# Seven products in place of eight for six K-tile pairs of the last down projection

## The reference

```python
def conv_ffn(h, w_up, conv_w, conv_b, w_down):     # D_MODEL 2048, D_FF 5632
    u = causal_depthwise_conv(h @ w_up, conv_w, conv_b)
    val, gate = jnp.split(u, 2, axis=-1)
    return (jax.nn.gelu(gate) * val) @ w_down      # (256 x 5632) @ (5632 x 2048), added to x
```

## Time and profile before

| | |
|---|---|
| three runs | 2272.08, 2274.09, 2274.53 us (median 2274.09) |
| span of the profiled execution, first to last instruction | 2272.6 us |
| own time of the profiled execution | not listed apart from the runs; the median is 1.5 us above its span |
| last section, first matmul | 2029.93 us from the start of the span |
| TensorE busy, mean granted clock | 2264.1 us (100%), 0.999 |
| VectorE, ScalarE, GpSimd busy | 1502.4, 1268.4, 619.1 us |

### The profile page before, as it was taken

The page is one execution under the profiler, slowest core; times in us unless marked ns, Lnnn a source line. Parts: engine busy times, 40 slices in busy tenths (PEclk is TensorE's granted clock), DMA queues, the critical chain, the costliest instruction groups (busy, mean ns, idle before and its releaser), DMA issues.

```text
span 2272.6 us, 33897 instructions
## 1 busy us (share of the span) xinstructions
PE 2264.1 (100%) x11072; PEld 1911.0 (84%) x11072; DVE 1502.4 (66%) x1812; ACT 1268.4 (56%) x1663; POOL 619.1 (27%) x1027
## 2 busy tenths in 40 slices
PE   9999999999999999999999999999999999999999
PEld 7888888988888888888888888898888888888887
DVE  6766775676767667665556778658767767665443
ACT  6655664565556555544444777556655655554333
POOL 0720001234343343412221100215434344340000
PEclk9999999999999999999999999999999999999999
DMA  8655435547776776766665555636867676776555
GB/s 274 207 199 200 133 126 176 176 151 219 217 223 214 222 222 213 222 206 202 203 203 188 174 193 175 200 126 216 253 220 221 216 223 212 221 221 193 194 193 167
DMA packets 143779, 455.24 MB, mean 200 GB/s; under 512 B 25888, under 2 KB 26784, under 8 KB 143696
## 3 DMA queue, kind: packets, MB, share of 16 engines
q1 hardware_dynamic: 117696, 420.40, 58.0%
q0 software_dynamic: 25856, 33.65, 4.9%
q10 hardware_dynamic: 144, 0.06, 0.0%
HBM read 423.73 MB, written 2.10 MB: 187 GB/s over the span
## 4 chain that ended last, share of the span: by engine, by line
PE 99%; ACT 0%; DVE 0%; DMA 0%; issue 0%; SPq 0%; ACTq 0%
PE ps L412 50%; PE ps L417 25%; PE ps L370 10%; PE ps L374 5%; PE ps L355 2%; PE ps L391 2%; PE ps L729 1%; PE ps L978 1%; PE ps L715 0%; PE ps L809 0%; PE ps L698 0%; PE ps L637 0%; DMA xT<-in_x_t 0%; PE ps L691 0%; PE ps L830 0%
## 5 line engine op out<-in xcount | busy, mean ns | idle before, releaser
L343 DVE TENSOR_TENSOR w_lo<-raw,w_hi 128x1024 fp32r<-128x1024 f32 x788 | 978.8, 1245 | 702.4 <-ACT w_hi L337 699.6
L337 ACT ACTIVATE w_hi<-raw 128x1024 fp32r<-128x1024 f32 x787 | 830.8, 1059 | 855.7 <-PE ps L417 738.7
L412 PE MATMUL ps<-w_hi,xg_hl 128*128 128x512 f32 (+1 forms) x3392 | 832.9, 388 | 1.9 <-DVE xg_hl L1462 1.9
L412 PEld LDWEIGHTS ps<-w_hi,xg_hl 128*128 128x128 f32 x3392 | 631.8, 188 | 131.4 <-DVE xg_hl L1462 2.4
L417 PE MATMUL ps<-w_lo,xg_hl 128*128 128x512 f32 (+1 forms) x1696 | 450.1, 388 | 0.0
L412 PE MATMUL ps<-w_hi,a_hl 128*128 128x512 f32 x1656 | 411.9, 391 | 0.3 <-ACT vmem L1110 0.2
L417 PEld LDWEIGHTS ps<-w_lo,xg_hl 128*128 128x128 f32 x1696 | 317.0, 188 | 65.3
L412 PEld LDWEIGHTS ps<-w_hi,a_hl 128*128 128x128 f32 x1656 | 308.8, 188 | 65.0 <-issue 0.7
L2140 POOL DMA_DIRECT2D u_t<-z_t x704 | 346.5, 500 | 2.8 <-issue 2.8
L417 PE MATMUL ps<-w_lo,a_hl 128*128 128x512 f32 x828 | 221.4, 389 | 0.0
L417 PEld LDWEIGHTS ps<-w_lo,a_hl 128*128 128x128 f32 x828 | 155.4, 188 | 32.5
(11 more groups left out here) (215 smaller groups left out, 1779.2 us busy)
## 6 DMA issues: line engine op xcount, KB each, us to landing
raw<-in_w_stream SPq DMA_DIRECT2D x787, 512.0 KB, 4.2
u_t<-z_t POOLq DMA_DIRECT2D x704, 34.0 KB, 3.4
bias<-in_rel_bias POOLq DMA_DIRECT2D x4, 768.0 KB, 5.8
memT<-in_mem_t POOLq DMA_DIRECT2D x4, 512.0 KB, 6.0
gate_w<-in_gate_w POOLq DMA_DIRECT2D x4, 512.0 KB, 3.8
x_tok<-x_turned SPq DMA_DIRECT2D x16, 128.0 KB, 4.3
out_t<-x_tok SPq DMA_DIRECT2D x8, 256.0 KB, 4.3
u_dn<-z_dn POOLq DMA_DIRECT2D x48, 32.0 KB, 3.2
```

What stands on the lines that cost most here:

```text
L337: nc.scalar.activation(w_hi[:, s, :], raw[:, s, :], ACT.Copy).then_inc(hi_done, 1)
L343: nc.vector.tensor_tensor(w_lo[:, s, :], raw[:, s, :], w_hi[:, s, :].bitcast(F), ALU.subtract).then_inc(lo_done, 1)
L412: nc.tensor.matmul(ps[:, bank + tt, 0:n], a[:, k0 + k, tt * P:tt * P + P], w_hi[:, s, k * n:k * n + n], start=start and k == 0 and q == 0, ...
```

## The change

For six of the 22 pairs (pairs 0 to 5, K-tiles 0 to 11) the two column blocks of a half q (blocks 2q and 2q+1) are computed together. The 2 x 2 x 2 = 8 block products (two token halves, two K-tiles, two column blocks) are replaced by the seven products of a Winograd form. GpSimd makes sums and differences of the activations' token halves (`forms`, three batches of two pairs each: one instruction that adds `a_hi` and `a_lo` over 1024 elements, then four over 256), ScalarE and VectorE split them. VectorE makes the sums of weight tiles (`weight_sums`, four instructions of 512). A paired step has four splits in place of two: one whole unit, half a unit and two summed tiles, and 21 matmuls in place of 24. After each half VectorE adds four more PSUM banks to the result (`product_sums`), with one copy by ScalarE. The units are reordered (`LAST_ORDER`): in the first half pairs 6 to 10 come first, then a paired step (`s`) after every two ordinary pairs (`c`, two units each); in the second half pairs 6 and 7 come first. Both blocks of a half now accumulate at the same time, block 2q in banks 0 and 1, block 2q+1 in banks 2 and 3, and the seven products in these and in banks 4 to 7.

```diff
+PAIRED = 6
+LAST_ORDER = [[("c", u) for u in range(6, 11)] + [x for j in range(5) for x in (("s", j), ("c", 11 + 2 * j), ("c", 12 + 2 * j))] + [("s", 5), ("c", 21)],
+              [("c", 6), ("c", 7)] + [x for j in range(PAIRED) for x in (("s", j), ("c", 8 + 2 * j), ("c", 9 + 2 * j))] + [("c", 20), ("c", 21)]]
+FORMS_AT = {6: 0, 14: 1, 22: 2}
...
+                if kind == "c":
+                    SPLITS += [("w", c), ("w", c + 1)]
+                else:
+                    SPLITS += [("w", c), ("h", c + 1), ("t", n, 0), ("t", n, 1)]
+                    RAW_OF[n] = c
...
+        SUMS_AT = {WSUM_SPLIT[PAIRED * (q + 1) - 1, 1] + SLOTS + j: (q, j) for q in range(2) for j in range(3)}
+        SUM_BEFORE = {SPLIT_OF[c]: n for n, c in RAW_OF.items()}
+        ADDS_AT = {e + b + SLOTS: (2 * q + b, e + b) for q, kind, u, e, _ in LAST if u == TOK_DOWN - 1 for b in range(2)}
...
+        def last_hi(act, e):
+            s, x = e % SLOTS, SPLITS[e - first["down1"]]
+            cols = slice(COLS if x[0] == "h" else 0, UE)
+            if x[0] == "t":
+                act.wait_ge(wsum_ready, 2 * x[1] + x[2] + 1)
+                src = t_raw[:, x[2], :]
+            else:
+                act.wait_ge(raw_full[x[1] % SLOTS], 16 * (x[1] // SLOTS + 1))
+                src = raw[:, x[1] % SLOTS, cols]
+            act.wait_ge(pe_unit, e - SLOTS + 1)
+            nc.scalar.activation(w_hi[:, s, cols], src, ACT.Copy).then_inc(hi_done, 1)
...
+                    if j % 2 == 0:
+                        pe.wait_ge(form_lo, min(n // 2, PAIRED // 2 - 1) + 1)
+                    if j == 0:
+                        if n:
+                            pe.wait_ge(sum_done, 1)
+                        else:
+                            pe.wait_ge(up_out, TT * 4 * UP_ITER)
+                    work = (((first_cols, a_part(0, 0), 4), (second_cols, a_part(1, 0), 0)),
+                            ((second_cols, s_part(3), 2),),
+                            ((first_cols, s_part(0), 5), (second_cols, s_part(1), 6)),
+                            ((first_cols, s_part(2), 7), (second_cols, a_part(1, 1), 1)))
+                    for x, products in enumerate(work):
+                        pe.wait_ge(hi_done, e + x + 1)
+                        for cols, form, bank in products:
+                            product(e + x, cols, form, bank, j == 0 and bank >= 4, False, None)
+                        pe.wait_ge(lo_done, e + x + 1)
+                        for cols, form, bank in products:
+                            last = product(e + x, cols, form, bank, False, j == PAIRED - 1 and bank >= 4, True)
+                        last.then_inc(pe_unit, 1)
...
+                for q, kind, u, e, n in LAST:
+                    if kind == "s":
+                        paired(u, e, n)
+                        continue
+                    begin, end = u == PAIRED, u == TOK_DOWN - 1
+                    for b in range(2):
+                        if q and b and end:
+                            continue
+                        token_unit(pe, e + b, 2 * u, 2, a_hi, a_lo, 2 * b, begin, end, value_there if q == 0 and b == 0 else None,
+                                   (lambda tt, b=b: pe.wait_ge(tile_done, 2 * b + tt + 1)) if q and begin else None)
...
+                last_hi(act, e)
+                if pos < 9:
+                    value_slot(1, UP_ITER, pos)
+                if pos in FORMS_AT:
+                    b = FORMS_AT[pos]
+                    act.wait_ge(form_made, b + 1)
+                    A(s_hl[:, 2 * b:2 * b + 2, :, 0, :].rearrange("p a f n -> p (a f) n"),
+                      s_f[:, 2 * b:2 * b + 2, :, 1, :].rearrange("p a f n -> p (a f) n"), ACT.Copy).then_inc(form_hi, 1)
...
+                ch.link(dve, V.tensor_tensor(t1, b12, b11, ALU.subtract))
+                V.tensor_tensor(t2, b22, t1, ALU.subtract).then_inc(wsum_ready, 1)
+                V.tensor_tensor(t3, b22, b12, ALU.subtract)
+                dve.wait_ge(wsum_ready, 2 * n + 1)
+                V.tensor_tensor(t4, b21, t2, ALU.subtract).then_inc(wsum_ready, 1)
...
+                if part == 0:
+                    dve.wait_ge(p1_out, q + 1)
+                    ch.link(dve, V.tensor_tensor(x_tok[:, n0, 0, :], x_tok[:, n0, 0, :], u_sum[:, :], ALU.add))
+                    ch.link(dve, V.tensor_tensor(u_sum[:, :], u_sum[:, :], ps[:, 6, :], ALU.add))
+                    ch.link(dve, V.tensor_tensor(x_tok[:, n1, 0, :], x_tok[:, n1, 0, :], u_sum[:, :], ALU.add))
+                if part == 1:
+                    ch.link(dve, V.tensor_tensor(u_sum[:, :], u_sum[:, :], ps[:, 7, :], ALU.add))
+                    x = x_tok[:, n0:n1 + 1, 1, :]
+                    ch.link(dve, V.tensor_tensor(x, x, u_sum[:, :].unsqueeze(1).to_broadcast([P, 2, COLS]), ALU.add))
+                if part == 2:
+                    x = x_tok[:, n1, :, :]
+                    ins = V.tensor_tensor(x, x, ps[:, 5, :].unsqueeze(1).to_broadcast([P, TT, COLS]), ALU.add)
+                    ins.then_inc(sum_done, 1)
+                    dve.wait_ge(sum_done, q + 1)
...
+                for e in range(c0 + SLOTS, END + SLOTS):
+                    pos = e - SLOTS - c0
+                    if e in SUMS_AT:
+                        q, part = SUMS_AT[e]
+                        dve.wait_ge(pe_unit, WSUM_SPLIT[PAIRED * (q + 1) - 1, 1] + 1)
+                        product_sums(q, part)
+                    if e in ADDS_AT and ADDS_AT[e][0] < 3:
+                        n, done = ADDS_AT[e]
+                        dve.wait_ge(pe_unit, done + 1)
+                        tile_adds(n)
+                    if e in SUM_BEFORE:
+                        weight_sums(SUM_BEFORE[e])
+                    if e < END:
+                        last_lo(dve, e)
+                    if pos < 9:
+                        value_slot(1, UP_ITER, pos)
+                    if pos in FORMS_AT:
+                        b = FORMS_AT[pos]
+                        dve.wait_ge(form_hi, b + 1)
+                        V.tensor_tensor(s_hl[:, 2 * b:2 * b + 2, :, 1, :].rearrange("p a f n -> p (a f) n"),
+                                        s_f[:, 2 * b:2 * b + 2, :, 1, :].rearrange("p a f n -> p (a f) n"),
+                                        s_hl[:, 2 * b:2 * b + 2, :, 0, :].rearrange("p a f n -> p (a f) n").bitcast(F), ALU.subtract).then_inc(form_lo, 1)
...
+            def forms(b):
+                if b == 0:
+                    pool.wait_ge(pe_unit, first["down1"])
+                    pool.wait_ge(g_lo, UP_ITER + PAIRED // 2)
+                ch.link(pool, G.tensor_tensor(a_f[:, 4 * b:4 * b + 4, :, 0, :],
+                                              a_hi[:, 4 * b:4 * b + 4, :].rearrange("p k (t n) -> p k t n", t=TT).bitcast(F),
+                                              a_lo[:, 4 * b:4 * b + 4, :].rearrange("p k (t n) -> p k t n", t=TT).bitcast(F), ALU.add))
+                a11, a21, a12, a22 = (s_f[:, 2 * b:2 * b + 2, f, 0, :] for f in range(4))
+                s1, s2, s3, s4 = (s_f[:, 2 * b:2 * b + 2, f, 1, :] for f in range(4))
+                ch.link(pool, G.tensor_tensor(s1, a21, a22, ALU.add))
+                ch.link(pool, G.tensor_tensor(s2, s1, a11, ALU.subtract))
+                G.tensor_tensor(s3, a11, a21, ALU.subtract)
+                G.tensor_tensor(s4, a12, s2, ALU.subtract).then_inc(form_made, 1)
+            def last_section():
+                for b in range(PAIRED // 2):
+                    forms(b)
...
+            down = down[[TOK_DOWN * (2 * q + b) + u for q in range(2) for _, u in LAST_ORDER[q] for b in range(2)]]
```

More of the change, by code:

```diff
@@ L145, in trunk @@
         rb = at("rb", top[0], [TT, P])
+        u_sum = at("u_sum", top[0], [COLS])
         sq = sb("sq", [SEQ])
@@ L269, in trunk @@
         out_done = sem("out_done")
+        form_made, form_hi, form_lo = sem("form_made"), sem("form_hi"), sem("form_lo")
+        wsum_ready, p1_out, sum_done = sem("wsum_ready"), sem("p1_out"), sem("sum_done")
         chains = {n: Chain(sem(f"{n}_self")) for n in ("act", "dve", "pool")}
@@ L281, in trunk @@
         N_UNITS = c
+        LAST, SPLITS, RAW_OF = [], [], {}
+        c, n = first["down1"], 0
+        for q in range(2):
+            for kind, u in LAST_ORDER[q]:
+                LAST.append((q, kind, u, first["down1"] + len(SPLITS), n))
+                if kind == "c":
[3 more added lines that the diff above has]
+                    RAW_OF[n] = c
+                    n += 1
+                c += 2
+        assert c == N_UNITS
+        END = first["down1"] + len(SPLITS)
+        SPLIT_OF = {x[1]: first["down1"] + j for j, x in enumerate(SPLITS) if x[0] != "t"}
+        WSUM_SPLIT = {(x[1], x[2]): first["down1"] + j for j, x in enumerate(SPLITS) if x[0] == "t"}
+        SUMS_AT = {WSUM_SPLIT[PAIRED * (q + 1) - 1, 1] + SLOTS + j: (q, j) for q in range(2) for j in range(3)}
+        SUM_BEFORE = {SPLIT_OF[c]: n for n, c in RAW_OF.items()}
```

(64 more changed lines are left out.)

22 lines of the change are left out of this document (11 added, 11 removed).

## The result

The changed kernel takes 2282.8 us (median of nine runs), the kernel before 2273.8 in runs beside it: ratio 1.0042, 95% interval 1.003 to 1.0053. That is 9.0 us more; 2283.0 was forecast. By that interval the change costs 6.8 to 12.1 us. The profiled execution took 2285.5 us, 2.7 more than the median (span 2283.8, mean granted clock 0.996).

What follows compares the result with a forecast made beforehand. The prediction took TensorE, busy all the span, to bound the kernel. -8.2 (matmuls) + 12.3 (start) + 1.75 (clock) + 3.0 (turn) = +8.9 on 2274.1 gave 2283.0 us, range 2269.5 to 2289.

Steps and rivals of the forecast that it cites:

- What goes: Twelve paired steps with 21 matmuls for 24: 36 matmuls fewer at 0.227 us each, -8.2 us.
- The regular stretch at nothing: In the cycles of a paired step and four ordinary units, slack of 1.7 us or more hides the added work: no cost.
- The start, +12.3: At the section's first paired step, VectorE and GpSimd alternate one instruction each, so TensorE starts it 12.3 us late.
- overlap (0.8): Rival at the start: the engines don't disturb each other, 0.8 us late and no clock loss, 2269.7 us in all; chance 0.13.
- VectorE keeping its turn (6.2): Rival at the start: VectorE keeps its turn while it has work, 6.2 us late, 2276.9 us in all; chance 0.15.
- The clock, +1.75: Behind the pause at the start the granted clock falls once, losing 1.75 us; bounds 0 and 3.5.
- The turn, +3.0: Between the halves TensorE waits for banks to be added, 2.1 us for block 0 and 0.9 for block 1: +3.0 us.
- The sum: Matmuls, start, clock and turn over the whole kernel: +8.9 us, giving 2283.0 us.

Runs made afterwards that it cites:

- cleared: `late_start` with the blocks' banks added first at the turn, GpSimd's batches and the forms' splits moved to where VectorE has slack: 2265.2 us, ratio 0.9964.
- spread_forms: Changed kernel with GpSimd's second and third batch of forms waiting for the section's 12th and 20th split: 2274.6 us, ratio 1.0001.
- late_spread_turn: `late_start` with the blocks' banks added first at the turn and GpSimd's later batches waiting as in `spread_forms`: 2269.0 us, ratio 0.9981.
- memset_forms: Changed kernel with GpSimd's fifteen forms instructions replaced by memsets of the same outputs, which read nothing (output wrong): 2269.1 us, ratio 0.998.
- filled_gap: Changed kernel with 50 matmuls whose result nobody reads run in the gap before the first paired step: 2279.8 us, ratio 1.003.
- late_start: Changed kernel with seven pairs in place of five ahead of the first half's first paired step: 2274.8 us, ratio 1.0009.

## Why the prediction was right

**What goes.** 36 matmuls, 8.2 us. Confirmed: the account closes with 8.16. In `cleared`, where nearly only this is left, the section is 6.1 us shorter with 2.05 of excess in it, and the medians are 7.5 apart.

**The regular stretch at nothing.** Confirmed: there is no wait in it afterwards, and the account leaves nothing over. The size of the slack was not measured; it held until `spread_forms` and `late_spread_turn` put GpSimd's batches into these cycles, and then TensorE waited.

**The start, +12.3.** Measured 11.91. The mechanism was the one named, turns of one instruction each: a pair of small instruction and multiply-add was put at 0.87, and eight multiply-adds with seven small and one long GpSimd instruction between them took 8.78, where the prediction's turns give 7 x 0.87 + 2.68 = 8.77. Two rivals fall by the trace of the changed kernel: overlap (0.8) and VectorE keeping its turn (6.2). `memset_forms` shows that GpSimd costs this only where it reads, and `spread_forms` that the cost hangs on where its batches fall.

The Trainium skill ("SBUF — State Buffer", section Who interferes with whom) says that a VectorE instruction with two inputs in SBUF meets a GpSimd instruction that reads SBUF, not one that only writes. Both halves agree with this case: 8.78 us against 3.25 for the same eight instructions.

**The clock, +1.75.** Right mechanism, size too small: 2.95 at the first paired step. It was taken from a stretch of the kernel's start that lost 1.75; here 2.95 lost at half the clock stand for 5.9 us at the low level (0.50 in the first two stretches above). `filled_gap` isolates it. The clock fell a second time, at the turn, which the sum doesn't have. Together both falls cost 4.6 us by my estimate (2.95, and 1.65 of the 1.83 at the turn, after about 0.18 of wait for the second bank as in `filled_gap`), more than the bound of 3.5.

**The turn, +3.0.** The first wait was 2.05, where the working gives 12.1 - 10.2 = 1.9. In all the turn cost 3.88 in this execution. Of the two gaps that were to show, the second is missing here: block 1's adds end at about 2167.1, and the slowed first unit of the half itself ends only at 2167.29. In `filled_gap`, where the clock stayed, both show, and what is left of its excess after the start (12.20) and 0.14 for the paired step is 15.46 - 12.34 = 3.1 us. So the banks' order costs the 3.0 of the sum, and the rest is the clock's.

**The sum.** The profiled execution lost 10.6 in the section where 8.9 was forecast: 0.4 less at the start, 1.2 more at the first paired step, 0.9 more at the turn. The medians are 9.0 apart, and that they meet the forecast within 0.1 is luck: the interval of 6.8 to 12.1 can't tell 8.9 from 10.6. The mean clocks of the nine executions run from 0.994 (2292.2 us) to 0.998 (2281.2 and 2281.7 us), so they differ in what they lost to the clock; where in the kernel the others lost it is not shown.

## What to carry to other kernels

An engine with nothing to do is not free help: before work goes to it, look in the trace for a stretch in which it and its neighbour both compute, and price each of the neighbour's instructions there at a whole turn of the other. Place such work by the slack of the engine it disturbs, and when the step that waits for it is moved, look at all the other work that meets the same company, since each piece has its own deadline. When two accumulations come to end together, empty first the banks that are wanted first.

## What the runs showed of the hardware that was not expected

The clock after a short pause is not settled by the pause's length. In the changed kernel an idle time of 1.9 us at the turn was followed by a granted clock of 0.85 and 0.53 in the first two stretches below, and in `memset_forms` by 0.83 and 0.54. The same 1.9 us in `filled_gap`, `spread_forms` and `late_start`, and 3.5 us in `spread_forms`, left it at 1.00. Idle times of 1.0 and 3.6 us a few us apart in `late_start` were followed by 0.61 over six us (2066 to 2072). What decides it is open. Changed kernel, then `memset_forms`:

```profile
2163.00:2165.00 2.00, 1.96 (x7) 1.52 (x8) 2.00 (x3) 0.00 (x0) 0.00 (x0) 0.85 0.06 23
2165.00:2168.00 3.00, 3.00 (x9) 2.27 (x8) 2.97 (x4) 0.41 (x1) 0.00 (x0) 0.53 0.56 175
```
```profile
2146.60:2148.60 2.00, 2.00 (x7) 1.54 (x8) 2.00 (x3) 0.00 (x0) 0.00 (x0) 0.83 0.02 6
2148.60:2151.60 3.00, 3.00 (x9) 2.29 (x8) 2.97 (x4) 0.48 (x1) 0.00 (x0) 0.54 0.57 175
```
